# Second attention of a two-block kernel: weights turned inside the next projection chunk, convolution input projected first

## The reference

```python
u = modulate(rmsnorm_2(h, g_mix), sh2, sc2)
qa, ka, va, xm, o_pre, ga, gb = split(u @ w_in)          # seven parts of 1024 columns
p = softmax(mask(rope(q) @ rope(k).T * scale))           # 8 heads, 2 parts each, query blocks of 128
a = p[:, 0] - lam * p[:, 1]
ya = rmsnorm_2(a @ v, g_subln) * (1 - lambda_init)
xc = silu(causal_conv(xm, conv_w, conv_b))               # 4 taps per channel
yb = mlstm(q=xc @ w_mq, k=xc @ w_mk, v=xm @ w_mv, ...) gated by o_pre
merged = sigmoid(ga) * (ya @ w_proj_a) + sigmoid(gb) * (yb @ w_proj_b)
h = h + gt2 * (merged @ w_out)
```

## Time and profile before

| | |
|---|---|
| median of 3 runs | 2096.04 us (2094.53 to 2097.24) |
| the profiled execution's own time | 2097.44 us |
| its span in the profile | 2095.6 us |
| granted TensorE clock, mean of the span | 0.97 |
| TensorE busy | 1986.1 us |
| VectorE busy | 1140.1 us |
| ScalarE busy | 781.1 us |
| GpSimd busy | 400.4 us |
| first projection matmul of unit 0 | at 1183.95 us |
| first QKV matmul after the loop | at 1446.60 us |

### The profile page before, as it was taken

How to read it: one execution, slowest core, us unless ns; L and a number is a source line. 1 busy time by engine, 2 the same in 40 slices (tenths; PEclk the granted TensorE clock), 3 DMA queues, 4 the chain that set the end, 5 groups by cost and what they waited for, 6 DMA issues and landing times.

```text
span 2095.6 us, 25549 instructions
## 1 busy us (share of the span) xinstructions
PE 1986.1 (95%) x9570; PEld 1596.1 (76%) x9570; DVE 1140.1 (54%) x1717; ACT 781.1 (37%) x1328; POOL 400.4 (19%) x334
## 2 busy tenths in 40 slices
PE   7998799999999999999999999988898999999996
PEld 6885477888887788888788877766566778888885
DVE  5557358666657665454554354566524655354443
ACT  5435532222234322222332355546645432222222
POOL 3000009999300595000000000042001000000000
PEclk8998899999999999999999999999999999999998
DMA  5330026666431564333254333323115423333231
GB/s 153 81 77 21 20 83 220 192 207 210 130 101 52 173 208 140 100 90 91 81 145 123 111 121 106 98 84 115 59 63 167 145 71 91 100 100 98 86 96 50
DMA packets 275143, 233.60 MB, mean 111 GB/s; under 512 B 16679, under 2 KB 248482, under 8 KB 274520
## 3 DMA queue, kind: packets, MB, share of 16 engines
q1 hardware_dynamic: 255216, 164.19, 27.0%
q0 software_dynamic: 18224, 62.91, 9.5%
q10 hardware_dynamic: 1624, 5.45, 1.1%
HBM read 215.41 MB, written 12.58 MB: 109 GB/s over the span
## 4 chain that ended last, share of the span: by engine, by line
PE 85%; DVE 7%; ACT 5%; issue 2%; DMA 0%; POOL 0%; ACTq 0%; SPq 0%; DVEq 0%
PE bank L1049 26%; PE bank L1051 25%; PE bank L1050 25%; DVE wlo L1669 1%; PE bank L1585 1%; ACT whi L514 1%; PE bank L1209 1%; ACT arena L730 1%; PE bank L1603 1%; PE bank L1316 1%; PE bank L1461 1%; PE bank L1580 1%; ACT arena L894 1%; PE bank L1469 1%; PE bank L1101 1%
## 5 line engine op out<-in xcount | busy, mean ns | idle before, releaser
L1049 PE MATMUL bank<-xhi,whi 128*128 128x512 f32 x1768 | 701.8, 397 | 21.5 <-DVE xlo L1675 10.1
L1050 PE MATMUL bank<-xlo,whi 128*128 128x512 f32 x1768 | 693.5, 392 | 0.0
L1051 PE MATMUL bank<-xhi,wlo 128*128 128x512 f32 x1768 | 693.4, 392 | 0.0
L1669 DVE TENSOR_TENSOR wlo<-stage,whi 128x1024 fp32r<-128x1024 f32 x309 | 410.5, 1339 | 229.6 <-ACT whi L514 229.1
L514 ACT ACTIVATE whi<-stage 128x1024 fp32r<-128x1024 f32 x309 | 321.2, 1051 | 415.8 <-PE bank L1051 384.4
L1049 PEld LDWEIGHTS bank<-xhi,whi 128*128 128x128 f32 x1768 | 335.3, 190 | 100.0 <-issue 27.1
L1051 PEld LDWEIGHTS bank<-xhi,wlo 128*128 128x128 f32 x1768 | 335.1, 190 | 71.6
L1050 PEld LDWEIGHTS bank<-xlo,whi 128*128 128x128 f32 x1768 | 335.5, 190 | 68.2
L1990 DVE SCALAR_TENSOR_TENSOR H<-bank,sc,H 128x512 f32<-128x512 f32 x304 | 219.2, 749 | 81.5 <-PE bank L1051 81.0
L1049 PE MATMUL bank<-hidhi,whi 128*128 128x512 f32 x608 | 241.5, 397 | 4.5 <-DVE hidlo L2015 4.4
L1051 PE MATMUL bank<-hidhi,wlo 128*128 128x512 f32 x608 | 238.5, 392 | 0.0
(11 more groups left out here) (403 smaller groups left out, 1850.9 us busy)
## 6 DMA issues: line engine op xcount, KB each, us to landing
arena<-in_w_ada POOLq DMA_DIRECT2D x72, 512.0 KB, 4.0
stage<-in_w_in SPq DMA_DIRECT2D x71, 512.0 KB, 3.9
stage<-in_w_ff SPq DMA_DIRECT2D x64, 512.0 KB, 4.5
stage<-in_w_gate SPq DMA_DIRECT2D x44, 512.0 KB, 4.5
stage<-in_w_up SPq DMA_DIRECT2D x44, 512.0 KB, 3.8
stage<-in_w_down SPq DMA_DIRECT2D x44, 512.0 KB, 3.8
arena<-arena ACTq DMA_DIRECT2D x16, 256.0 KB, 5.3
stage<-in_w_proj_a SPq DMA_DIRECT2D x8, 512.0 KB, 4.0
```

What stands on the lines that cost most here:

```text
L1049: mm(out, sh, mh, start=start, stop=False, **kw)
L1050: mm(out, sh, ml, start=False, stop=False, **kw)
L1051: return mm(out, sl, mh, start=False, stop=stop, **kw)
L1669: V.tensor_tensor(wlo[:, static % SPLITS, :], stage[:, static % STAGES, :], whi[:, static % SPLITS, :].bitcast(F32), ALU.subtract).then_in ...
```

## The change

`SIDE` now begins with the eight `xm` chunks, so the convolutions lie in units 1 to 8 in place of 25 to 32; `XM0 = 0` is where they begin. TensorE turns unit i-1's weights between the fourth and the fifth k-tile of chunk i, no longer unit i's after it. ScalarE copies the turned weights of unit i-1 (`mixed_out`) ahead of the copy of chunk i and, in group units, behind the group's squares; the eight Silu stand in unit 31 behind the copy for unit 30, ahead of the copy of chunk 31. VectorE normalises a group after its unit's weights. GpSimd's convolution takes a buffer of `gg` as its temporary for tiles 0 and 2 and waits for the rotations where it needs their places; group 1's squares wait for it.

```diff
-SIDE = [("ga", 5 * D + P * j) for j in range(8)] + [("gb", 6 * D + P * j) for j in range(8)] + \
-       [("op", 4 * D + P * j) for j in range(8)] + [("xm", 3 * D + P * j) for j in range(8)]
+SIDE = [("xm", 3 * D + P * j) for j in range(8)] + [("ga", 5 * D + P * j) for j in range(8)] + \
+       [("gb", 6 * D + P * j) for j in range(8)] + [("op", 4 * D + P * j) for j in range(8)]
+XM0 = 0
...
 # ScalarE
-                if n >= 26:
-                    act.wait_ge(s("conv" if n % 2 else "conv_even"), (n - 24) // 2)
+                if XM0 + 2 <= n < XM0 + KT + 2:
+                    act.wait_ge(s("conv" if n % 2 else "conv_even"), (n - XM0) // 2)
...
                 act.wait_ge(s("av_group"), g + 1)
+                if g == 1:
+                    act.wait_ge(s("conv_even"), 2)
...
+            def mixed_out(i):
+                b = i // AH
+                act.wait_ge(s("at_t"), i + 1)
+                if i >= 2:
+                    act.wait_ge(s("av_done"), i - 1)
+                A_(amT[i % 2][:, 0:b + 1, :], bank[4][:, 0:(b + 1) * P].rearrange("p (b q) -> p b q", q=P), ACT.Copy).then_inc(s("amt_out"), 1)
...
                 if ph == 0 and 0 <= g < 7:
                     group_squares(g)
+                if i:
+                    mixed_out(i - 1)
+                if i == UNITS - 1:
+                    for kt in range(KT):
+                        act.wait_ge(s("conv" if kt % 2 else "conv_even"), kt // 2 + 1)
+                        A_(E[:, kt, :], E[:, kt, :], ACT.Silu).then_inc(s("xc_ready"), 1)
                 if i < UNITS:
                     act.wait_ge(chunk_done, C_SIDE + i + 1)
                     store_side(i, bank[6][:, :])
-                    act.wait_ge(s("at_t"), i + 1)
-                    if i >= 2:
-                        act.wait_ge(s("av_done"), i - 1)
-                    A_(amT[i % 2][:, 0:b + 1, :], bank[4][:, 0:N].rearrange("p (b q) -> p b q", q=P), ACT.Copy).then_inc(s("amt_out"), 1)
...
-            for kt in range(KT + 1):
-                if kt < KT:
-                    act.wait_ge(s("conv" if kt % 2 else "conv_even"), kt // 2 + 1)
-                    A_(E[:, kt, :], E[:, kt, :], ACT.Silu).then_inc(s("xc_ready"), 1)
-                if kt:
-                    act.wait_ge(s("xc_ready"), kt)
-                    split_hi(5, kt - 1, E[:, kt - 1, :])
+            for kt in range(KT):
+                act.wait_ge(s("xc_ready"), kt + 1)
+                split_hi(5, kt, E[:, kt, :])
...
 # TensorE
-            def project(c, out, static=None, filling=None):
+            def project(c, out, static=None, filling=None, between=None):
...
+                    if between is not None and kt == KT // 2:
+                        between()
...
-                    project(C_SIDE + i, bank[6][:, :]).then_inc(chunk_done, 1)
+                    project(C_SIDE + i, bank[6][:, :], between=(lambda: turn(i - 1)) if i else None).then_inc(chunk_done, 1)
                     if i + 1 < UNITS:
                         scores(i + 1)
-                    turn(i)
+                else:
+                    turn(i - 1)
...
 # VectorE
-                g, ph = divmod(i - 5, 4)
-                if ph == 0 and 0 <= g < 7:
-                    group_normalise(g)
                 if i < UNITS:
                     dve.wait_ge(s("at_exp"), i + 1)
...
-                if UNITS - KT < i <= UNITS and (i - (UNITS - KT) - 1) % 2:
-                    conv(i - (UNITS - KT) - 1)
+                g, ph = divmod(i - 5, 4)
+                if ph == 0 and 0 <= g < 7:
+                    group_normalise(g)
+                if XM0 < i <= XM0 + KT and (i - XM0 - 1) % 2:
+                    conv(i - XM0 - 1)
...
 # GpSimd
-                tmp = tabs[:, 0, 0:T]
+                tmp = gg[:, 1, 0:T] if n < 4 else tabs[:, 0, 0:T]
+                if n in (2, 4):
+                    pool.wait_ge(s("rot2_done"), 4 if n == 2 else 7)
```

More of the change, by code:

```diff
@@ L2120, in conv @@
                 x = outst[n % 2]
-                dve.wait_ge(s("side_out"), UNITS - KT + n + 1)
+                dve.wait_ge(s("side_out"), XM0 + n + 1)
                 w = lambda k: pc("conv_w_2", 8 * k + n)
```

## The result

The changed kernel takes 2099.73 us (median of 12 runs, 2094.45 to 2107.47) against 2096.51 us (12 runs of the kernel before, 2088.71 to 2097.67): a ratio of 1.0028, 95% interval 1.0015 to 1.004. It is slower, by 5.9 us as the ratio has it and 3.2 as the medians do. That is little, but the interval lies above 1; the forecast was 2 us faster.

What follows compares the result with a forecast made beforehand. TensorE, busy 95%, was taken as the bound, standing still mainly at both ends of the second attention for VectorE's weights; start +13.5, middle -1.8, end -12.1, QKV -1.4 gave -1.8 us, median 2094.2 us, range 2092 to 2099.

Steps and rivals of the forecast that it cites:

- Start, units 0 to 9: the convolution's new place: First ten units: VectorE's chain sets the pace with convolutions and GpSimd contention added; projection 10 starts 13.5 us later.
- 1.6 us of low clock ahead of unit 10: End of the start: TensorE's third wait, in unit 9, lowers its clock uncovered by VectorE, costing about 1.6 us.
- The rule that I weighed: Beside GpSimd, two-SBUF-input operations contend; rotations in units 1 and 4 would stretch some 2 us more, sum about zero.
- The waits: TensorE in units 3, 5 and 9: waits of some 4, 7 and 3 us, released by ScalarE's copies or group's values.
- The middle: Units 10 to 24: TensorE's 1.4 us of waits go, with a few tenths of unlisted slack: -1.8 us.
- the nearest row: Profile row of group 7's four transposes inside projection matmuls, 0.90 us for two steps; used to price interruptions at zero.
- One of my signs: Third block: projection periods over 7.7 us would show the forecast wrong.
- The end: Units 25 to QKV: no convolution left, Silu in one block, TensorE waits 3.1 us; 62.8 against 74.9 us, -12.1.
- QKV: QKV chunks: the second chunk's 1.42 us wait for ScalarE's first copy goes, -1.4 us.
- The start costs little: Rival, first ten units: convolutions and GpSimd interleave better, 8.7 us more gained, 2085.5 us; chance 0.31.
- The interruption is dear: Rival, all 31 mid-chunk turns: each costs TensorE 0.3 us, adding 9.3 us, 2103.5 us, slower; chance 0.19.

Runs made afterwards that it cites:

- no_pool_conv: Changed kernel with GpSimd's even-tile convolutions left out except eight columns of their first operation: 2086.83 us, ratio 0.9964 to the kernel before.
- apart_turn_outside: apart_silu3 with the turn back outside the projection chunk, in the unit of its own weights: 2101.95 us, ratio 1.0034 to the kernel before.
- apart_silu3: Changed kernel with `xm` chunks paired at units 9-10, 13-14, 17-18, 21-22, groups normalised before weights, three Silu ahead of chunk 31's copy: 2082.24 us, ratio 0.9931.

## Why the prediction was wrong

**The step that failed** is the price of contention in "Start, units 0 to 9: the convolution's new place": rotations and splits 25% longer, 0.5 us for each maximum, a convolution at 4.7 beside GpSimd's. In all it put 7.1 us on contention (4.7 on convolutions, 2.4 on the rest). The runs show 13.6. The other part of the start, what the place costs without GpSimd, I had at 13.5-7.1 = 6.4 us; no_pool_conv measures 79.45-72.98 = 6.5. That match is in part luck: my 6.4 holds 1.6 us of low clock ahead of unit 10, and in no_pool_conv unit 9 waits 1.07 us and unit 10 runs its 7.01 us at full speed; laps longer than mine make up for it. Laps from maximum to maximum, with the terms of the prediction (the group's 1.3 us is in units 6 and 9):

| unit | predicted | after | no_pool_conv |
|---|---|---|---|
| 2 | 11.5 | 13.35 | 9.63 |
| 3 | 7.3 | 7.29 | 6.77 |
| 4 | 11.8 | 13.03 | 9.61 |
| 5 and 6 | 17.0 | 16.57 | 16.06 |
| 7 | 5.5 | 7.51 | 6.48 |
| 8 | 8.3 | 8.58 | 8.23 |
| 9 | 6.7 | 6.66 | 6.67 |

Units 2, 4 and 7 are where GpSimd works on an even tile beside the weights and, in 2 and 4, the convolution: 5.5 us from its first to its last operation where I had 4.7, and the weights ahead of it, where I had put nothing. Of the 2.0 us in unit 7 half is contention; the lap is 6.48 even without it. Unit 1 has 2.0 us of contention for the 0.8 that I gave it. And one place wasn't in the sum at all: GpSimd's first tile already lies beside unit 0's weights, which ended 9.5 us after unit 0's start in place of the 8.3 that I took (1192.3 against 1183.95); 0.9 of the 1.2 is two operations, 0.16 to 0.84 and 0.35 to 0.60 us.

What misled me was reading the contention as a share of an operation's length. I had two measured shares, 1.42 for 0.77 and 25% on the split, and took the milder one for rotations and splits. It was an average of two kinds: in that stretch 28 splits take 1.21 to 1.23 us and 15 take 1.87 to 3.41. The row that showed the true form was among those I quoted: line 2112 at 1.27 us for four columns. I used it for one operation a lap, and for the wrong one: the maximum stays at 0.28, its negative (line 2153) pays. At half a GpSimd instruction (0.5 us), the mean found since, for each of the six VectorE operations beside it, the weights' too, the lap of unit 2 would have come out at 6.8+2.9+3.0 = 12.7; at a whole one it would have come out over 15. 

The rule that I weighed, of the Trainium skill ("GPSIMD Engine Reference", 8. Key points), names operations with two SBUF inputs and those in a two-port mode. I applied the first half to the rotations, worth 2 us, and left out the second. Whether TENSOR_SCALAR ran in such a mode no run shows, but the trace has it among the hardest hit.

**The waits** came where I put them (4.85, 8.06 and 3.00 us for 4, 7 and 3), released by ScalarE's copy and the group's values.

**The middle** was -1.8 and is +1.0. The waits did go. But the low clock after unit 9's wait, which I put at 1.6 us ahead of unit 10, falls inside unit 10 (8.98 us for 7.01), and 15 interruptions of 0.04 us are 0.65. I had them at nothing, by the nearest row. One of my signs was badly set: periods over 7.7 us in the third block are there (8.10 us in unit 20), but the kernel before has them too (8.01).

**The end** was -12.1 and is -12.9: last unit to QKV 12.14 us where I had 13.5, the six units before it 49.9 for 49.3, Silu in one block, 3.15 us of wait.

**QKV** was -1.4 and is -0.4. The 1.42 us gap is gone, but QKV now begins 1.5 us after the wait of 3.15, at the lower clock, which before lay on the value matmuls.

**The rivals.** "The start costs little" falls by every run: even without GpSimd it costs 6.5. "The interruption is dear" gave about the measured time and the right sign, by a mechanism that is not there: 31 times 0.04 us are 1.3, and at the largest difference of a single unit, 0.11, still 3.4, not 9.3. What I lacked as the case on the slower side was contention on every VectorE operation that works in SBUF beside GpSimd, 6.5 us more than my 7.1, which takes the sum near the result.

What stays open: which of the two engines gets its way when they meet, and so what an order of operations will cost. With the turn outside the chunk they meet more kindly, but no run varied the order alone. In unit 0 VectorE passed a GpSimd instruction, in unit 2 a like pair cost it 0.71 us.

## What to carry to other kernels

Work moved to an idle GpSimd is not free beside VectorE: count the VectorE operations in SBUF that run beside it, the smallest too, and charge each one about half a GpSimd instruction (0.48 us in the mean here, 1.1 at most), not a percentage. A mid-chunk turn gives room of half a chunk for 0.04 us, and it is worth that only where the lap it covers is late by less than the room: here less than nothing beside laps of 13 us in a row, 20 us beside single convolutions spread between other units. The turn alone measured as no difference, the spread placement without it as slower (apart_turn_outside, 1.0034), both together as 14.6 us faster, so try parts together in another placement before dropping either.

## What the hardware showed that I had not expected

For their length, VectorE's smallest operations are hit most by GpSimd: 128x2 elements 0.17 to 0.69 or 0.81 us, 128x1 0.16 to 0.84, 128x128 TENSOR_SCALAR 0.29 to 1.00 and 1.41, 128x512 0.54 to 1.59; the maximum out of PSUM stays at 0.28. Unchanged code ahead of unit 0 takes 1175.4 to 1184.6 us in different executions, as much as the whole effect of the change. And waits of 3.4 to 4.2 us cost TensorE nearly half as much again in the lower clock: 17.0 us of waits in the middle of *apart_turn_outside* against 2.0 at the group's transposes in *apart_silu3*, with 6.1 us more of busy time for the same matmuls.
